# Ring places by first release, home slabs behind two expert slabs, and four adaLN slabs inside the input projection

## What is computed

```python
for i in range(DEPTH):                      # DEPTH = 4
    mod = (silu(cond) @ w_ada[i] + b_ada[i])            # 1024 -> 6 * 1024
    sh1, sc1, g1, sh2, sc2, g2 = split(mod, 6)
    h = rmsnorm(x, norm_g[i, 0]) * (1 + sc1) + sh1
    y = mixer_i(h)          # 0: Hyena (h @ w_in, short convolution, two FFT convolutions, @ w_out)
                            # 1: gated linear attention (GLA)   2: 2-D DFT @ w_out   3: pooling
    x = x + g1 * y
    h = rmsnorm(x, norm_g[i, 1]) * (1 + sc2) + sh2
    x = x + g2 * hier_moe(h)   # 16 SwiGLU experts, best group of 4, best 2 in it
```

## Time and profile before

| | us |
|---|---|
| median of three runs | 1403.72 (1401.99 to 1403.74) |
| the profiled execution | 1400.19 |
| its span, first instruction to last | 1398.0 |
| TensorE busy | 1343.8 |
| VectorE busy | 473.5 |
| ScalarE busy | 286.2 |
| GpSimd busy | 32.1 |

### The profile page before, as it was taken

How to read it: one execution, slowest core, us unless ns; L and a number is a source line. 1 busy time by engine, 2 the same in 40 slices (tenths; PEclk the granted TensorE clock), 3 DMA queues, 4 the chain that set the end, 5 groups by cost and what they waited for, 6 DMA issues and landing times.

```text
span 1398.0 us, 17305 instructions
## 1 busy us (share of the span) xinstructions
PE 1343.8 (96%) x7140; PEld 743.5 (53%) x7140; DVE 473.5 (34%) x1067; ACT 286.2 (20%) x514; POOL 32.1 (2%) x30
## 2 busy tenths in 40 slices
PE   9999999999988899999999988999999999999996
PEld 4786585444434688775444424854444356444433
DVE  3787514111114797624112113141111144111113
ACT  3311024111103122224111103241111035111102
POOL 0001310000000000010000000100000000000000
PEclk9999999999999999999999999999999999999999
DMA  9997999999999995789999999889999998999995
GB/s 384 420 398 271 421 420 414 428 427 427 428 428 418 422 406 227 264 357 407 428 426 428 428 428 419 349 364 414 427 428 428 427 419 359 407 426 428 427 427 210
DMA packets 55654, 554.37 MB, mean 397 GB/s; under 512 B 6097, under 2 KB 8081, under 8 KB 9233
## 3 DMA queue, kind: packets, MB, share of 16 engines
q1 hardware_dynamic: 53792, 551.19, 94.7%
q10 hardware_dynamic: 1778, 2.01, 0.4%
HBM read 551.08 MB, written 2.10 MB: 396 GB/s over the span
## 4 chain that ended last, share of the span: by engine, by line
PE 79%; DMA 16%; DVE 2%; ACT 1%; SPq 1%; issue 0%; POOL 0%; DVEq 0%; POOLq 0%
PE bank L773 26%; PE bank L719 14%; PE bank L797 13%; DMA ring<-in_moe_w 10%; PE bank L738 5%; DMA ring<-in_w_ada 4%; PE bank L756 4%; PE bank L679 3%; PE bank L565 2%; DMA ring<-in_hy_w_in 2%; PE bank L693 2%; PE bank L549 1%; PE bank L1022 1%; PE bank L906 1%; PE bank L629 1%; PE bank L623 1%
## 5 line engine op out<-in xcount | busy, mean ns | idle before, releaser
L773 PE MATMUL bank<-ring,hT 128*64 128x512 f32 x1024 | 225.3, 594 | 0.0
L773 PE MATMUL bank<-ring,arena 128*64 128x512 f32 x896 | 199.6, 595 | 22.3 <-DMA ring<-in_moe_w 22.3
L797 PE MATMUL bank<-ring,arena 128*64 128x512 f32 x896 | 198.5, 595 | 0.0
L1533 DVE TENSOR_TENSOR rows<-rows,bank 128x512 f32<-128x512 f32 x32 | 22.0, 688 | 456.5 <-PE bank L773 456.5
L773 PEld LDWEIGHTS bank<-ring,hT 128*64 128x64 f32 x1024 | 72.1, 137 | 139.3 <-issue 137.6
L773 PEld LDWEIGHTS bank<-ring,arena 128*64 128x64 f32 x896 | 63.8, 137 | 150.7 <-issue 128.3
L797 PEld LDWEIGHTS bank<-ring,arena 128*64 128x64 f32 x896 | 61.7, 137 | 116.9 <-issue 115.2
L1552 DVE SCALAR_TENSOR_TENSOR yv_rest<-bank,arena,yv_big 128x512 fp32r<-128x512 f32 x64 | 48.0, 750 | 199.9 <-ACT yv_big L1221 199.9
L719 PE MATMUL bank<-hT,ring 128*128 128x256 f32 x512 | 112.0, 380 | 0.3 <-DMA ring<-in_hy_w_in 0.3
L719 PEld LDWEIGHTS bank<-hT,ring 128*128 128x128 f32 x512 | 96.6, 190 | 15.1 <-issue 2.2
L1221 ACT ACTIVATE yv_big<-bank,arena 128x512 fp32r<-128x512 f32 x64 | 44.0, 688 | 281.0 <-PE bank L797 281.0
(11 more groups left out here) (227 smaller groups left out, 1375.8 us busy)
## 6 DMA issues: line engine op xcount, KB each, us to landing
ring<-in_moe_w SPq DMA_DIRECT2D x152, 2048.0 KB, 18.5
ring<-in_w_ada SPq DMA_DIRECT2D x96, 1024.0 KB, 14.8
ring<-in_moe_w SPq DMA_DIRECT2D x48, 1024.0 KB, 23.6
arena<-in_moe_w SPq DMA_DIRECT2D x16, 1024.0 KB, 14.6
arena<-in_moe_w SPq DMA_DIRECT2D x8, 2048.0 KB, 9.7
ring<-in_hy_w_in SPq DMA_DIRECT2D x12, 1024.0 KB, 27.3
ring<-in_hy_w_out SPq DMA_DIRECT2D x4, 1024.0 KB, 14.0
ring<-in_gla_w_v SPq DMA_DIRECT2D x4, 1024.0 KB, 26.2
```

The source lines that it names most:

```text
L773: last = mm(bank[4 + kind][SLOTS * e:SLOTS * e + SLOTS, :], x[:, k, at:at + SLOTS], w[:, kk, e, :], start=k == 0, stop=k == KD - 1)
L797: last = mm(bank[6 + q // 2][SLOTS * e:SLOTS * e + SLOTS, :], hidT[:, f, SLOTS * e:SLOTS * e + SLOTS], w[:, ff, e, :], start=f == 0, stop= ...
L1533: tt(sil[:], sil[:], bank[5][:], ALU.mult).then_inc(s(pre + "hid_ready"), 1)
```

## The change

Three things are altered in the order and the placing of the slabs; what is computed stays the same.

1. `ring_places` takes the place of the running counter. It goes through the same list and gives each slab the place whose last slab is used earliest, by a table of estimated times of use (`use_order`, written by hand, in us from the start of the kernel or 1000 more per layer). A double takes the pair of places (even, odd) for which the later of both uses is earliest. The marker `cond_done` goes; `cond` has an estimated time of use like the others.
2. `("first", i)`, the four home slabs with their wait, stands behind the first two expert slabs of the layer instead of ahead of them.
3. Four slabs of third 2 are used inside the input projection, behind tiles 9, 13, 17 and 21, and stand in the list behind `w_in` 4, 6, 8 and 10. Between the transforms, thirds 2 and 3 are dealt out anew.

The fallback loop for further rounds of the experts uses places 0 to 11 by their numbers.

```diff
+    w_in = among("w_in", 12, 1, 0, KD, 2, 1.25)
+    for k in range(4):
+        w_in.insert(w_in.index(("w_in", 4 + 2 * k)) + 1, ("ada", 2, k))
-    before = [ada(0) + among("w_in", 12, 1, 0, KD, 2, 1.25) + ada(2) + ada(3) + ada(4) + pieces("w_out", 4) + ada(5),
+    before = [ada(0) + w_in + ada(2, 4) + ada(3) + ada(4) + pieces("w_out", 4) + ada(5),
...
-        for what in before[i] + [("first", i)] + experts + [("further", i)]:
-            if what[0] in ("first", "further"):
-                out.append((what, None, None))
-                at += at % 2
-                continue
...
-            if at % RING == held:
-                at += 1
-            if what[0] == "cond":
-                held = at % RING
-            out.append((what, at % RING, at // RING))
-            at += 1
+        for what in before[i] + experts[0:2] + [("first", i)] + experts[2:] + [("further", i)]:
+            out.append(what)
+    return ring_places(out)
+
+
+def use_order(what):
+
+    name, c = what[0:2]
+    if name == "moe":
+        _, i, p, kind, q = what
+        return 1000 * i + 400 + 25.7 * p + 9 * kind + 1.75 * (q + 1)
+    if name == "ada":
+        n, k = c, what[2]
+        if n == 0:
+            return 10 + 3.5 * k
+        if n == 1:
+            return 53 + 10 * k
+        if n == 2:
+            return 75 + 14 * k if TWO_EARLY and k < 4 else 126 + 2.5 * k
...
+    return {"w_in": 47 + 7 * c, "w_out": 190 + 7 * c, "cond": 1128, "wq": 1019 + 7 * c, "wk": 1038 + 7 * c,
+            "wv": 1052 + 7 * c + (2 * c if TWO_EARLY else 0), "wg": 1000 + (80, 111, 118, 140)[c % 4], "wo": 1168 + 7 * c,
+            "fn": 2018 + 7 * c, "pool": 3010}[name]
+
+
+def ring_places(order):
+
+    free, out = [-1.0] * RING, []
+    for n, what in enumerate(order):
+        if what[0] in ("first", "further") or homed(what):
+            out.append((what, None, None))
+            continue
+        if second_half(what):
+            slot = out[-1][1] + 1
+        elif in_halves(what):
+            slot = min(range(0, RING, 2), key=lambda m: (max(free[m:m + 2]), m))
+        else:
+            slot = min(range(RING), key=lambda m: (free[m], m))
+        free[slot] = use_order(what)
+        out.append((what, slot, None))
     return out
...
                 project(bank[m % 4][:, 0:NT], "w_in", m, "win_mm",
                         ready=(lambda k: h_ready(0, k)) if m == 0 else None)
+                if m in (9, 13, 17, 21):
+                    ada(2, (m - 9) // 4, (m - 9) // 4 + 1)
             pe.wait_ge(s("up_ready"), 24)
...
             to_rows(0)
-            ada(2, 0, 1)
+            ada(2, 4, 5)
             forward(0)
             to_rows(1)
-            ada(2, 1, 5)
+            ada(2, 5, 8)
             forward(1)
             inverse(0)
-            ada(2, 5, 8)
-            ada(3, 0, 3)
+            ada(3, 0, 4)
             to_rows(2)
             ada_turned(2)
-            ada(3, 3, 4)
+            ada(3, 4, 5)
             forward(2)
             inverse(1)
-            ada(3, 4, 8)
+            ada(3, 5, 8)
             ada(4, 0, 2)
```

More of the change, by code:

```diff
@@ L36 @@
 SLABS = 4
+TWO_EARLY = True
 ADAS = 3 * LAYERS
@@ L143, in piece_stream @@
               + wv[3:] + ada(7, 1, 2) + wg[0:1] + ada(7, 2, 4) + wg[1:2] + ada(7, 4, 6) + wg[2:3] + ada(7, 6, 7)
-              + wg[3:] + ada(7, 7) + ada(9) + pieces("wo", 4) + ada(10) + [("cond_done", 6)],
+              + wg[3:] + ada(7, 7) + ada(9) + pieces("wo", 4) + ada(10),
               pieces("fn", 4) + ada(11),
               pieces("pool", 1)]
-    out, at, held = [], 0, None
+    out = []
     for i in range(LAYERS):
@@ L150, in piece_stream @@
                    if p or kind < 2]
-        for what in before[i] + [("first", i)] + experts + [("further", i)]:
-            if what[0] in ("first", "further"):
-                out.append((what, None, None))
-                at += at % 2
-                continue
-            if homed(what):
-                out.append((what, None, None))
-                continue
-            if what[0] == "cond_done":
-                held = None
-                continue
-            if at % RING == held:
-                at += 1
-            if what[0] == "cond":
-                held = at % RING
-            out.append((what, at % RING, at // RING))
-            at += 1
+        for what in before[i] + experts[0:2] + [("first", i)] + experts[2:] + [("further", i)]:
+            out.append(what)
@@ new lines, in piece_stream @@
+    return ring_places(out)
[12 more added lines that the diff above has]
+            return 75 + 14 * k if TWO_EARLY and k < 4 else 126 + 2.5 * k
+        if n in (3, 4, 5):
+            return (146, 162, 212)[n - 3] + 2.3 * k
+        if n == 6:
+            return 1000 + (20, 25, 30, 38, 52, 55, 62, 67)[k]
+        if n == 7:
+            return 1000 + (72, 77, 82, 86, 108, 113, 118, 128)[k]
+        if n == 8:
+            return 1000 + (0, 1, 8, 9, 10, 28, 29, 30)[k]
+        if n == 9:
+            return 1000 + (142, 147, 153, 154, 160, 161, 162, 163)[k]
+        return (1192 if n == 10 else 2040) + 1.8 * k
+    return {"w_in": 47 + 7 * c, "w_out": 190 + 7 * c, "cond": 1128, "wq": 1019 + 7 * c, "wk": 1038 + 7 * c,
+            "wv": 1052 + 7 * c + (2 * c if TWO_EARLY else 0), "wg": 1000 + (80, 111, 118, 140)[c % 4], "wo": 1168 + 7 * c,
+            "fn": 2018 + 7 * c, "pool": 3010}[name]
@@ L512, in one_round @@
                             for q in range(SLABS):
-                                sp.dma_start(ring[where["moe", i, 1, kind, q][0]][:],
+                                sp.dma_start(ring[SLABS * kind + q][:],
                                              expert_slab(6 * (PAIRS * i + j) + 2 * kind + q // 2 + 12 * c, q)) \
@@ L874, in weights @@
                             pe.wait_ge(s(f"fb_full{kind}"), 16 * SLABS * (n + 1))
-                            return ring[where["moe", i, 1, kind, q][0]].rearrange("p (k n) -> p k n", k=2)
+                            return ring[SLABS * kind + q].rearrange("p (k n) -> p k n", k=2)
                         pe.wait_ge(s(pre + "hidT_ready"), primed(n))
```

## The result

| | before | after |
|---|---|---|
| median, us (lowest to highest) | 1402.18 (1400.64 to 1403.74) | 1406.34 (1404.14 to 1408.61) |
| profiled execution, us | 1400.19 | 1404.59 |
| its span, us | 1398.0 | 1402.4 |

The changed kernel takes 1.0029 times as long as before, interval 1.0018 to 1.0039: 4.1 us more (2.5 to 5.5). Forecast were 3.1 us more and 1406.8 us. So time and sign came out; the terms came out less well, and that is what the runs are about. That the forecast of the time itself lies nearer (1406.8 against 1406.34) than that of the difference is chance: it started from 1403.72 for the kernel before, which over more executions takes 1402.18.

What follows compares the result with a forecast made beforehand. Expert slab transfers were taken to bound each layer's end, from the last unavoidable hole in their stream. Terms 0.6 + 1.5 + 1.0 = 3.1 us on 1403.72 gave 1406.8 us, range 1401 to 1410.

Steps and rivals of the forecast that it cites:

- Layer 0, forecast +0.6: Early slabs delay w_out by 1.3 us, 0.7 us of head start survives; layer 0 ends 0.6 us later (-0.7 to +3.6).
- The slab's price: In the input projection, one adaLN slab between tiles takes TensorE 0.99 us, so the projection ends 4.0 us later.
- TensorE's waits of layer 0 absorb it: In layer 0, TensorE itself being 1.3 us later doesn't add, since its waits for slabs take it up.
- The landing rule: In layer 0, the slab taking w_out's last place lands no earlier than 5.0 us after issue, against 5.7 before.
- Layer 1, forecast +1.5: Layer 1's third double waits for a used neighbour place until 653.7, lands 7.7 us later; +1.5 us (-3.5 to +1.7).
- Layer 3, forecast +1.0: Layer 3's third double waits for the first expert slab until 1180.6; arena slab lands at 1207.9, +1.0 us (0 to 1.3).
- Home slabs, forecast 0: Two slabs, 4.9 us of transfers, go ahead of SyncE's 24.3 us wait in layer 2; neither cost nor gain, 0.
- Layer 2, forecast 0: In layer 2 the ring places only swap names, and the home slabs' later position gains nothing; 0.
- Whatever is won before 952 us is lost there: In layer 2, the arena double issued at about 952.6 already lands at the 7.7 us floor, so earlier gains vanish.
- The clock (rival 4): After TensorE's 4.4 us standstill, half clock loses 2.5 us; one stretch more (1409.3) or less (1404.3), chance 0.12 each.
- head start survives: Early slabs' 9.8 us of transfers would reach layer 0's end past w_out, giving 1396.4 us; chance 0.06.
- doubles find neighbours: In layers 1 and 3 doubles find two free places and cond's place pays; -2.9 us, 1400.8 to 1401; chance 0.08.

Runs made afterwards that it cites:

- run 1: The kernel before with only the four early adaLN slabs between input projection tiles; ratio 1.0016, 2.2 us above before.
- 3: The kernel before with only the places given back first (no early slabs, home slabs ahead); ratio 1.0063, 8.8 us above before.
- 5: The places alone on the kernel before, with adaLN 5's first slab told to take the third place given back; ratio 1.0011, 1.5 us above before.
- 2: The kernel before with only the home slabs put behind the first two expert slabs; ratio 1.0010, 1.4 us above before.
- 6: The changed kernel with 13 single slabs told other places so layer 1's third double finds neighbours; ratio 0.9989, 1.5 us below before.
- 4: The changed kernel with 15 single slabs told other places so the third doubles of layers 1 and 3 find neighbours; ratio 1.0002, 0.3 us above before.
- run 7: The changed kernel with the four early adaLN slabs used in one run behind tile 21; ratio 1.0096, 13.5 us above before.
- 11: The early slabs alone, places in turn, the four used in one run behind tile 21 and loaded ahead of w_in's last; ratio 1.0010, 1.4 us above before.
- 8: The changed kernel without early slabs, 12 single slabs told other places to leave neighbours in layers 0, 1 and 3; ratio 0.9991, 1.3 us under before.
- 10: The changed kernel with early slabs, neighbours in layer 1 and layer 3's first two slabs laid as neighbours; ratio 0.9992, 1.1 us under before.
- run 9: As run 8, without early slabs, but layer 3's first two slabs laid as neighbours; ratio 0.9983, 2.4 us under before.

## Why the prediction was right, and which of its terms were off

The total, 4.1 us against 3.1, rests on three terms that all had the right place and sign and were all too small. They add up to over 5 us, so that the total came out within 1 us is in part luck: the clock and the scatter between traces hide the rest.

- **Layer 0, forecast +0.6, measured +2.2** (the change's 2.7 less the 0.5 of its start; run 1 in all 2.2). Two steps failed. The slab's price was read from its start to the next start (0.99) and not from what it does to its neighbours' pace (1.19): 4 x 0.2 = 0.8 us. And "TensorE's waits of layer 0 absorb it" was wrong: the landings moved by 2.3 to 2.6 us, since the same shift of TensorE also moves the releases of places. The landing rule itself held: 5.0 us after w_out's last place, and at this slab the 0.7 us that I had put to the good were there (it lands 1.98 us later, TensorE stands 2.71 late). Behind it most of them are gone. The next single, issued with 3.5 us left to go of the one ahead (before 4.3), lands 3.30 us behind it and not 2.75, and a double issued with 3.6 us left (before 4.0) lands 5.8 us behind and not 5.5 (last section).
- **Layer 1, forecast +1.5.** The double's issue (653.7 and TensorE's 1.7 = 655.4; measured 655.59) and landing (7.7; 7.8) came out. In the traces without a half-speed stretch behind layer 1's experts the two first pairs stand 284.1 to 284.3 us apart with the late double (after, 3, 5), and 283.1 without it (2). Before and run 1 have 283.8 and 283.5, of which 1.7 us are the clock between 865 and 875. That puts the term between 1.0 and 2.4 us. The landings, which the clock behind them doesn't touch, put it closer: against TensorE's start of the first pair the first arena slab lands 3.33 - 1.68 = 1.65 us later than before in the changed kernel, and 1.7 and 1.6 us later in runs 3 and 5. Runs 6 and 4 show by undoing it that the place is the cause, and give back more than the term, since they also remove what held before.
- **Layer 3, forecast +1.0, measured 1.4** (220.6 against 219.2; runs 2, 3, 5, 6 and 7 with the late double 220.4 to 220.9, before and runs 1 and 11 with the early one 219.1 to 219.5). The issue came out (1180.6 and 3.0 = 1183.6; measured 1183.82). The landing of the arena slab behind it didn't: 9.7 us after its issue where I had let the queue run on at 4.9 us each. It costs 0.8 us, by the effect told in the last section.
- **Home slabs, forecast 0.** In the changed kernel nothing points to more: layer 2's two slabs land 9 to 10 us earlier and the slab paced by fn still lands 5.1 us after its issue. Run 2's 1.4 us are what layer 3's place costs (1.3 in its trace), and not the home slabs' time.
- **Layer 2, forecast 0, in the trace +1.0** (247.6 us from its first pair to layer 3's, before 246.5). The arena slab that is issued at 954.56 takes 8.8 us where the one of before takes 7.7. Other traces speak against the home slabs and the places as its cause: runs 2 and 3 have 246.5, and run 1, which has neither, 247.7. The 13 traces lie between 246.3 and 249.1 (run 4, with its 3.4 us of low clock); what makes the difference is open.
- **"Whatever is won before 952 us is lost there" was wrong.** Runs 6 and 8 win 3.4 and 4.1 us between the first pairs of layers 1 and 2 and stand 0.5 and 4.3 us ahead of before at layer 2's (run 6 came 2.9 late); at layer 3's it is 0.7 and 3.8. (Of run 8's 4.1, 1.7 are the clock.) The arena slab at 952 stands at its floor, but its issue is released by TensorE, so it moves with it (948.26 in run 8, though it then takes 9.8 us and not 7.7, and lands 2.3 us earlier than before). A floor behind a release that TensorE itself gives passes a gain on; only a release of fixed time would stop it.
- **The clock (rival 4) did have a hand in it.** In these traces the losses come in amounts of 1.7 and 3.4 us. The one behind layer 0 is 3.4 before and 1.7 after, which the ruler shows as -1.0, and before loses 1.7 between 865 and 875 where after loses none. The terms alone make 2.2 + 1.0 to 2.4 + 1.4 = 4.6 to 6.0 us (5.3 with the landings' 1.65); 4.1 were measured. More than one profiled execution speaks for the clock: over 84 executions of before the mean granted clock is 0.9945, over 9 of the changed kernel 0.9966, which is 7.7 and 4.8 us lost of 1402 and 1406. But a lost microsecond costs the whole less than one: among the 84 the time falls by only 0.5 us for each 0.001 of clock, which is 1.4 us lost. So between 1 and 3 us of the change's cost are hidden by the clock, and how many isn't shown. All nine kernels with `ring_places` lose less than before and its in-turn variants (4.7 to 6.7 against 6.8 to 7.7 us) except that run 7 comes level with run 1; whether it is the table of places that does this, and how, isn't shown. The Trainium skill, TensorE: Matmul & The Clock Gate, Part 1, has the array slow after an idle stretch: the trace agrees at 475 us, but not for run 4 at 1165, where the two rows show TensorE busy for all 10 us; the largest idle time near it is 0.7 us, at 1155.
- The rivals "head start survives" and "doubles find neighbours" fell as they were set out: 5.0 us of landing at 212.5 (rival 1), issues at 655.59 and 1183.82 (rival 2). What I hadn't asked is how near the table was to something worse: without the early slabs one place in layer 0 costs 7 us (run 3 against run 5).

What stays open: layer 2's 1.0 us; how much the clock hides, in the change and in run 5 (it loses 5.6 us by its mean clock, before 7.7, which may be why its ratio is small); and, in layer 3 of runs 8 to 10 (220.1 to 221.7 us from first pair to end, before 219.2), what is left beyond the late fourth or fifth double: its arena slab lands 1.2 to 1.8 us later against TensorE, and the traces differ from before by 0.9 to 2.5.

## What to carry to other kernels

When transfers of two sizes share a ring, the place that comes free first is not the best place: give a single slab the place that leaves pairs whole, and write down for each double which use releases it, in each layer. An order of issue fixed in a list turns every wrong due time into a stall of the whole queue, so a table of due times has to be changed together with the order of use. And price an inserted piece of work by how far the next release slides, not by its own length.

## What the runs showed of the hardware

**A transfer issued shortly before the queue runs dry is late.** For the doubles (2 MiB) of the second to seventh pairs in the 13 traces, but for 39 that stand right behind a small transfer, I took how long the transfer ahead still had to go at the issue (its landing less the issue), and the time from issue to landing:

| left to go at the issue | doubles | us from issue to landing, median (range) | behind the landing ahead by over 5.2 us |
|---|---|---|---|
| under 1.7 us, or landed | 26 | 7.7 (7.5 to 7.9) | 26 of 26 |
| 2.2 to 4 us | 33 | 9.4 (7.6 to 9.9) | 29 of 33 |
| 4 to 4.7 us | 33 | 9.2 (8.9 to 10.5) | 9 of 33 |
| 4.7 to 6 us | 64 | 10.5 (9.6 to 12.0) | 4 of 64 |
| over 6 us | 1677 | 18.8 (10.8 to 33.0) | 62 of 1677 |

In a full queue doubles land 4.89 us apart. One issued with 3 us left to go ought to land 7.9 us after its issue and takes 9.4: no less than if it had been issued 1.5 us after that and had then taken its 7.7. So an issue that is earlier by so much can gain nothing. Layer 3's arena slab shows it: with 2.4 us left it takes 9.6 in run 9, with 0.9 left 7.7 in run 1. Sometimes the transfer ahead takes the extra time and not the late one, as in layer 3 of the changed kernel (spacings of 5.74 and 4.90 at the last two). The cause isn't shown. The Trainium skill, DMA: Bandwidth & Descriptors, section Anatomy of one DMA, puts a fixed 2.0 us on each DMA besides its transfer, most of it the confirmation of the write. It is for GpSimd's path; its fit would give an estimated 6.8 us for 2 MiB, where SyncE's take 7.7 here. No run here shows where in the 7.7 us the overlap goes wrong.

**Entering another kind of matmul costs about 0.2 us** beyond the slab's own start-to-start time: 1.19 against 0.99 for one slab between tiles, 3.77 against 3.57 for four in a run.

**The start of an execution varies by up to 1.3 us** before anything that was changed is reached, so terms under 1 us can't be read from one profiled execution, only from many kernels that share them. All of it arises in one row of TensorE in the first 10 us, and from there on the shift stays the same to w_in (before, then run 2, which is 1.05 us late):

```profile
4.35 4.26 PE L896 MATMUL bank<-ones 128*128 128x128 f32 x24
4.35 5.30 PE L896 MATMUL bank<-ones 128*128 128x128 f32 x24
```

The view gives the granted clock as 1.00 there in both, so the cause isn't shown.
